# Moving the normalised row to PSUM, handing far adds to TensorE and cutting the last gate into quarters in a YOCO trunk with PEER experts

## The reference

```
h = rmsnorm(x, ffn_norm)                         # HP
a = einsum('tkd,td->tk', u[idx], h)              # 128 experts per token: the "dots"
x = x + einsum('tk,tkd->td', gate * gelu(a), v[idx])      # the "adds"
g = sigmoid(rmsnorm(x, ple_norm) @ ple_wg)       # the gate
x = x + g * (p @ ple_wp)
out = rmsnorm(x, final_norm)
```

## Time and profile before

| | us |
|---|---|
| median of 3 runs | 2817.46 |
| lowest and highest | 2817.01, 2819.46 |
| the profiled execution, its own time | 2819.06 |
| its span, first to last instruction | 2817.3 |
| busy in the span: PE, DVE, ACT, POOL | 2283.0, 2131.1, 1091.4, 1244.0 |
| mean granted TensorE clock | 0.94 |

### The profile page before, as it was taken

The page is one execution under the profiler, slowest core; times in us unless marked ns, Lnnn a source line. Parts: engine busy times, 40 slices in busy tenths (PEclk is TensorE's granted clock), DMA queues, the critical chain, the costliest instruction groups (busy, mean ns, idle before and its releaser), DMA issues.

```text
span 2817.3 us, 22875 instructions
## 1 busy us (share of the span) xinstructions
PE 2283.0 (81%) x6632; PEld 1170.4 (42%) x6632; DVE 2131.1 (76%) x4499; ACT 1091.4 (39%) x3193; POOL 1244.0 (44%) x1042
## 2 busy tenths in 40 slices
PE   7887669877799878887677898899867797768777
PEld 5545225342335534554253355456524342223222
DVE  5897888878777767768888887686797887675445
ACT  3442334324344334632324343363332435333333
POOL 2444444434444344543544544354343444444334
PEclk8999989999899999999889999899998999989999
DMA  9999999999999999999999999999999999999996
GB/s 363 415 402 420 420 420 419 419 416 420 417 394 420 420 420 414 419 420 420 420 418 418 416 380 420 419 410 420 420 420 419 419 410 420 420 400 421 419 420 267
DMA packets 163646, 1157.53 MB, mean 411 GB/s; under 512 B 18360, under 2 KB 20536, under 8 KB 26048
## 3 DMA queue, kind: packets, MB, share of 16 engines
q0 software_dynamic: 148416, 1073.81, 92.4%
q1 hardware_dynamic: 14528, 80.43, 7.0%
q10 hardware_dynamic: 576, 1.84, 0.2%
HBM read 1153.90 MB, written 2.10 MB: 410 GB/s over the span
## 4 chain that ended last, share of the span: by engine, by line
DMA 43%; PE 29%; DVE 19%; ACT 5%; issue 3%; POOL 1%; DVEq 0%; ACTq 0%; POOLq 0%
DMA slot<-in_uv,idx 42%; PE acc L1041 15%; DVE slot L1805 8%; DVE X L1793 2%; PE B L791 2%; PE M L663 2%; PE B L663 2%; POOL slot L631 1%; PE M L791 1%; ACT diag L1283 1%; PE M L982 1%; ACT w L1275 1%; PE B L982 1%; ACT act_a L1273 1%; DVE top_u L1417 1%
## 5 line engine op out<-in xcount | busy, mean ns | idle before, releaser
L1041 PE MATMUL acc<-slot,diag 128*128 128x512 f32 x2968 | 1509.5, 645 | 478.3 <-ACT diag L1283 477.3
L631 POOL DMA_INDIRECT slot<-in_uv,idx x1012 | 1212.2, 1198 | 1535.2 <-PE acc L1041 1082.5
L1805 DVE CUSTOM_DVE_ANT_0 slot<-slot,HP 128x1024 f32<-128x1024 f32 x1024 | 1242.0, 1220 | 535.1 <-DMA slot<-in_uv,idx 516.8
L1041 PEld LDWEIGHTS acc<-slot,diag 128*128 128x128 f32 x2968 | 557.4, 201 | 1316.9 <-ACT diag L1283 778.3
L1273 ACT ACTIVATE act_a<-a 128x1 f32<-128x1 f32 x1024 | 208.4, 204 | 1563.9 <-DVE a L1805 1557.8
L1793 DVE SCALAR_TENSOR_TENSOR X<-slot,w,X 128x1024 f32<-128x1024 f32 x276 | 353.6, 1281 | 13.3 <-ACT w L1275 13.2
L1275 ACT ACTIVATE w<-act_a,gate 128x1 f32<-128x1 f32 x1012 | 300.8, 297 | 33.0
L1283 ACT ACTIVATE diag<-cst,w 128x128 f32<-128x128 f32 x736 | 296.9, 403 | 23.8
L1805 DVE DVE_READ_ACCUMULATOR2_ANT a<- 128x1 f32 x1024 | 83.8, 82 | 0.0
L1273 ACT ACT_TABLE_LOAD x57 | 73.1, 1283 | 9.1 <-DVE a L1805 8.1
L791 PE MATMUL M<-TT,w 128*128 128x256 f32 x320 | 72.8, 384 | 0.0
(11 more groups left out here) (233 smaller groups left out, 1734.8 us busy)
## 6 DMA issues: line engine op xcount, KB each, us to landing
w<-in_wq SPq DMA_DIRECT2D x18, 1024.0 KB
slot<-in_uv,idx POOLq DMA_INDIRECT x1012
w<-in_w_o SPq DMA_DIRECT2D x8, 1024.0 KB
w<-in_w_dq SPq DMA_DIRECT2D x6, 1024.0 KB
w<-in_w_uq_nope SPq DMA_DIRECT2D x8, 768.0 KB
KV<-in_ple_wg SPq DMA_DIRECT2D x5, 1024.0 KB, 19.5
slot<-in_wq SPq DMA_DIRECT2D x4, 1024.0 KB, 12.5
KV<-in_wq SPq DMA_DIRECT2D x4, 1024.0 KB, 16.6
```

Of the source, the lines that this page charges most:

```text
L631: nc.gpsimd.indirect_dma_start(out=slot[s][:, 0:width], out_offset=None, in_=uv[g // NC] if n < GATHERS - LATE else near, in_offset=bass.I ...
L1041: last = nc.tensor.matmul(acc[:, half * 512:half * 512 + 512], diag[adds_on_pe(n) % DIAGS][:], slot[s][:, D + half * 512:D + half * 512 + ...
L1805: nc.vector.tensor_tensor_reduce(out=slot[s][:, 0:D], in0=slot[s][:, 0:D], in1=HP[:, :], scale=1.0, scalar=0.0, op0=ALU.mult, op1=ALU.add, ...
```

## The change

From row `HP_MOVES` = 936 on, ScalarE copies HP to the PSUM tile T, and the dots from row 945 on read T in place of HP. The near half of row 1023 is added by VectorE and not by TensorE. The far halves of rows 1017 and 1018 (`FAR_ON_PE`, 5 and 6) are gathered first and added by TensorE to the far half of `acc`, whose sum into X moves from before the last dot to the middle of the tail; VectorE makes the other ten far adds behind both copies of the first half's transposes. Transposes and their copies go in quarters of 256 columns, into the two halves of T in turn. The gate's columns go in three groups, 0:512, 512:768 and 768:1024, the last into `acc`; the sum of squares of the third group is made by VectorE, and the bias of the root in two steps. The diff leaves out the counts of semaphores per stage and the wider tile of single values.

```diff
@@ -54,6 +54,11 @@
 DESCRIPTORS = 2048
 ROWS = 64
 WARM, WARM_AGAIN, WARM_LAST = 11, 3, 5
+FAR_ON_PE = (5, 6)
+FAR_ORDER = FAR_ON_PE + tuple(i for i in range(LATE) if i not in FAR_ON_PE)
+HP_MOVES = GATHERS - KSEL + 40
+TAIL_COLUMNS = ((0, 512), (512, 768), (768, 1024))
+QUARTER_AT = (0, 512, 256, 768)
 STEP = "step"
 
 C_IDENT, C_MASK, C_IOTA, C_INV, C_EPS = 0, P, 2 * P, 2 * P + TOPK, 2 * P + TOPK + HALF
@@ -305,7 +310,7 @@
 def on_dve(n):
 
     g, k = divmod(n, KSEL)
-    return n < GATHERS - LATE and PLACED[g][1][k] == "D"
+    return n == GATHERS - 1 or (n < GATHERS - LATE and PLACED[g][1][k] == "D")
 
 
 DVE_DONE = [0]
@@ -543,6 +548,8 @@
         dve_steps = sem("dve_steps")
         half_summed, hat_scaled, half_gated, half_added = (sem("half_summed"), sem("hat_scaled"), sem("half_gated"),
                                                            sem("half_added"))
+        gate_sums = dict(zip(TAIL_COLUMNS, (M[:, 0:512], M[:, 512:768], acc[:, 0:256])))
+        hp_moved, columns_multiplied = sem("hp_moved"), sem("columns_multiplied")
         out_squared, out_biased, out_rooted = sem("out_squared"), sem("out_biased"), sem("out_rooted")
         trig_shifted, trig_done = sem("trig_shifted"), sem("trig_done")
         copied = (m_copied, b_copied)
@@ -634,7 +641,7 @@
                     ).then_inc(rows_loaded[s], 16)
             pool.wait_ge(weights_used, used("ple_wp", PAIRS - 2, 0))
             pool.wait_ge(last_embedded, 1)
-            for i in range(LATE):
+            for i in FAR_ORDER:
                 k = KSEL - LATE + i
                 nc.gpsimd.indirect_dma_start(
                     out=late_rows[i], out_offset=None, in_=far,
@@ -998,14 +1005,37 @@
             def tail_stage(g0, n):
                 t0 = before("t_copied", "tail", g0)
                 pe.wait_ge(t_copied, t0)
+                for i in FAR_ON_PE:
+                    pe.wait_ge(late_loaded[i], 16)
+                    nc.tensor.matmul(acc[:, 512:D], diag[adds_on_pe(GATHERS - LATE + i) % DIAGS][:], late_rows[i],
+                                     start=False, stop=(i == FAR_ON_PE[-1])).then_inc(pe_added, 1)
+                wg = [piece("ple_wg", g0, i) for i in range(4)]
+
+                def gated(k, lo, hi):
+
+                    at = (k % 4) * 512 + lo % 512
+                    return nc.tensor.matmul(gate_sums[lo, hi], TT[:, k, 0:P], wg[2 * (lo // 512) + k // 4][:, at:at + hi - lo],
+                                            start=(k == 0), stop=(k == DB - 1))
+
                 for half in range(2):
                     pe.wait_ge(half_summed, half + 1)
-                    transposes(X[:, g0 % NC, half * 512:half * 512 + 512], 4, at=half * 512).then_inc(t_filled, 1)
+                    for quarter in (2 * half, 2 * half + 1):
+                        at = quarter * GW
+                        transposes(X[:, g0 % NC, at:at + GW], 2, at=QUARTER_AT[quarter]).then_inc(t_filled, 1)
                     if half == 0:
-                        warm(5, M, ident)
-                    pe.wait_ge(t_copied, t0 + half + 1)
-                    for i in (half, half + 2):
-                        half_product(0, i, piece("ple_wg", g0, i)).then_inc(weights_used, 1)
+                        warm(2, M, ident)
+                        for quarter in range(2):
+                            pe.wait_ge(t_copied, t0 + quarter + 1)
+                            for lo, hi in TAIL_COLUMNS:
+                                for k in (2 * quarter, 2 * quarter + 1):
+                                    gated(k, lo, hi)
+                    else:
+                        for lo, hi in TAIL_COLUMNS:
+                            for k in range(4, DB):
+                                if lo == 0 and k % 2 == 0:
+                                    pe.wait_ge(t_copied, t0 + k // 2 + 1)
+                                last = gated(k, lo, hi)
+                            last.then_inc(columns_multiplied, 1)
                 yield
 
             def add_stage(g0, n):
@@ -1041,7 +1071,8 @@
                     last = nc.tensor.matmul(acc[:, half * 512:half * 512 + 512],
                                             diag[adds_on_pe(n) % DIAGS][:],
                                             slot[s][:, D + half * 512:D + half * 512 + 512],
-                                            start=(n == mine[0]), stop=(n == (whole if half else mine)[-1]))
+                                            start=(n == mine[0]),
+                                            stop=(n == (whole if half else mine)[-1] and not (half and g == PAIRS - 1)))
                 last.then_inc(pe_added, 1)
                 if n == GATHERS - WARM_LAST:
                     wait_mb("tail", PAIRS - 1, 1)
@@ -1234,20 +1265,20 @@
                 yield from norms("tail", g0, rows(g0, 1), D)
                 nc.scalar.activation(out_rms[:, 0:1], ident[:, 0:1], ACT.Sigmoid)
                 act.wait_ge(hat_scaled, 1)
-                for half in range(2):
-                    at = slice(half * 512, half * 512 + 512)
-                    act.wait_ge(weights_used, used("ple_wg", g0, 2 + half))
-                    nc.scalar.activation(A[:, 0, at], M[:, at], ACT.Sigmoid,
+                for j, (lo, hi) in enumerate(TAIL_COLUMNS):
+                    act.wait_ge(columns_multiplied, j + 1)
+                    nc.scalar.activation(A[:, 0, lo:hi], gate_sums[lo, hi], ACT.Sigmoid,
                                          scale=rstd[:, norm_number("tail", g0):norm_number("tail", g0) + 1]
                                          ).then_inc(half_gated, 1)
-                    if half:
-                        nc.scalar.activation(out_rms[:, 0:1], out_ss[:, 0:1], ACT.Sqrt)
-                    act.wait_ge(half_added, half + 1)
-                    nc.scalar.activation(sq_out[:, at], X[:, c, at], ACT.Square, accum_out=out_ss[:, half:half + 1]
-                                         ).then_inc(out_squared, 1)
-                    act.wait_ge(out_squared, half + 1)
-                act.wait_ge(out_biased, 1)
-                nc.scalar.activation(out_rms[:, 1:2], out_ss[:, 1:2], ACT.Sqrt, bias=out_bias[:, 0:1], scale=1.0 / D
+                    if j < 2:
+                        act.wait_ge(half_added, j + 1)
+                        nc.scalar.activation(sq_out[:, lo:hi], X[:, c, lo:hi], ACT.Square, accum_out=out_ss[:, j:j + 1]
+                                             ).then_inc(out_squared, 1)
+                act.wait_ge(out_squared, 2)
+                nc.scalar.activation(out_rms[:, 0:1], out_ss[:, 0:1], ACT.Sqrt)
+                act.wait_ge(out_squared, 3)
+                act.wait_ge(out_biased, 2)
+                nc.scalar.activation(out_rms[:, 1:2], out_ss[:, 2:3], ACT.Sqrt, bias=out_bias[:, 1:2], scale=1.0 / D
                                      ).then_inc(out_rooted, 1)
                 act.wait_ge(out_ready, NC)
                 act.dma_start(out[c * P:(c + 1) * P, 0:D // 2], outs[c][:, 0:D // 2]).then_inc(out_stored, 16)
@@ -1269,6 +1300,10 @@
                 s = n % SLOTS
                 if k in ranks_of(g):
                     act.wait_ge(gate_ready, before("idx_ready", ranks_of(g)[k], g) + 1)
+                if n == HP_MOVES:
+                    act.wait_ge(t_copied, before("t_copied", "tail", g))
+                    act.wait_ge(hp_ready, before("hp_ready", "renorm", g) + 1)
+                    nc.scalar.activation(T[:, :], HP[:, :], ACT.Copy).then_inc(hp_moved, 1)
                 act.wait_ge(dotted_or_added, DOTS[n])
                 nc.scalar.activation(act_a[:, s:s + 1], a[:, s:s + 1], ACT.Gelu_apprx_tanh).then_inc(gelued, 1)
                 act.wait_ge(gelued, n + 1)
@@ -1729,37 +1764,51 @@
                     return nc.vector.scalar_tensor_tensor(X[:, c, halves[1]], late_rows[i], weight_of(n),
                                                           X[:, c, halves[1]], ALU.mult, ALU.add)
 
-                for i in range(2):
-                    step(add_far(i))
+                near_half, far_half = halves
                 dve.wait_ge(pe_added, adds_on_pe(GATHERS - 1))
-                nc.vector.tensor_tensor(X[:, c, halves[0]], X[:, c, halves[0]], acc[:, halves[0]], ALU.add
-                                        ).then_inc(half_summed, 1)
-                for i in range(2, 4):
-                    step(add_far(i))
-                for half in range(2):
-                    dve.wait_ge(t_filled, before("t_filled", "tail", g0) + half + 1)
-                    nc.vector.tensor_tensor(TT[:, 4 * half:4 * half + 4, 0:P],
-                                            T[:, half * 512:half * 512 + 512].rearrange(blocks, t=P),
-                                            columns(G_PLE + DB + 4 * half, 4), ALU.mult).then_inc(t_copied, 1)
-                    if half == 0:
-                        for i in range(4, LATE - 1):
+                dve.wait_ge(dotted_or_added, added_by(GATHERS - 1))
```

(44 more changed lines are left out.)

8 lines of the change are left out of this document (4 added, 4 removed).

## The result

The changed kernel takes **2824.73 us**, the median of 12 runs (2821.43 to 2826.47); the kernel before, measured beside it, 2818.72 (12 runs, 2817.01 to 2820.49). The ratio is 1.0021 with a 95% interval of 1.0012 to 1.0029: slower by 6.0 us, just over the 5.6 us that the prediction set as the bound for no change. Forecast were 2818.6, a range of 2816.2 to 2821.6, and a chance of 0.05 for slower.

A forecast was written before the change was run, and what follows sets the result against it. Gathered rows (DMA) bound the kernel until the last rows are in, then VectorE's tail chain. Terms of +0.97 us (last dot to last far add's end) and +0.19 (to the root) took the median 2817.46 to 2818.6; range 2816.2 to 2821.6.

The forecast's parts named there:

- the terms of the sum: Tail behind the last dot: +0.97 us up to the last far add's end, +0.19 from there to the root; +1.2 together.
- part 1: HP's copy to PSUM at row 936 costs 0; dots reading PSUM cost 0, at most 0.1 us.
- freed, it would be some four us earlier. That is worth 0: GpSimd's last far issue in the tail comes some four us earlier, worth 0 as VectorE reaches that row after 2800.0.
- The first item of part 2: Behind the last dot, VectorE waits for TensorE's add of row 1022: start 2788.36, 1.12 long, so 2789.5.
- Rival (a): TensorE idles 2.5 us before the second products, clock falls to 0.50 for 3.4 us; 1.1 to 1.7 us lost; chance 0.33.
- Rival (e): Dots slower with an operand in PSUM, over the twelve near rows; slower by over 0.2%, 2828 at twice the length; chance 0.03.
- The ends of part 2: From the last dot to the last far add's end: near sum, copies, ten far adds at 0.88; end at 2802.4, +0.97 us.
- H: Instant the last far add ends, before which nothing of the last gate's second half can start; forecast 2802.4, +0.97 us.
- Part 3: From the last far add's end to ScalarE's last root, with quarters and three column groups: 12.14 against 11.95, +0.19 us.
- rival (b): Quarters in the tail leave only 256 columns' work behind the last product; 1.4 us less than before, 2817.0; chance 0.12.
- (c): Landings of far rows, not VectorE, set the last far add's end, and freed GpSimd pays; 2817.5 to 2818; chance 0.06.
- (d): HP's copy does not free GpSimd; last landing 2800.0, time 2818.6 as forecast; no chance of its own given.

The follow-up runs named there:

- e6: Changed kernel with twelve idle products keeping TensorE busy before the second half's transposes; 2820.09 us, ratio 1.0006.
- e5: Changed kernel, unaltered, measured again in the second group; 2821.44 us, ratio 1.0008.
- f1: Changed kernel, unaltered, measured again in the fourth group; 2824.62 us, ratio 1.0020.
- f5: f6 with far gathers 2 to 9 on GpSimd each held until a dot of rows 1016 to 1023 is done; 2819.62 us, ratio 1.0003.
- f6: The kernel of e6 again (changed kernel, TensorE kept busy by idle products), in the fifth group; 2823.97 us, ratio 1.0020.
- e3: Kernel before with only the move of HP to PSUM, late dots reading T; 2818.64 us, ratio 1.0003.
- e1: Changed kernel with all twelve far adds on VectorE, none on TensorE; 2822.35 us, ratio 1.0015.
- e2: Changed kernel with HP left in SBUF, all dots reading HP; 2820.38 us, ratio 1.0008.
- e11: Changed kernel with two far adds ahead of the first copies, HP in SBUF, ScalarE's squares behind the next sigmoid; 2817.74 us, ratio 0.9998.
- first and second group: Variants of the changed kernel taking parts back, then variants testing TensorE's granted clock, on one chip; kernel before 2818.29 and 2818.89 us.
- e8: Changed kernel with HP left in SBUF and idle products keeping TensorE busy before the second half; 2818.56 us, ratio 1.0000.
- f2: The kernel of e3 again (kernel before with only HP moved to PSUM), in the fourth group; 2821.97 us, ratio 1.0009.
- f3: Changed kernel with GpSimd holding each far gather until the one two before it has landed; 2830.39 us, ratio 1.0037.

## Why the prediction was wrong

An estimate of where the 6.0 us come from, from medians of the later groups: the terms of the sum, +1.2 (e6 against before, no pause and no clock fall); the clock fall, 1.35 (e5 against e6); the pause, 3.3 to 4.35 (f1 against e5, each over its own before; f5 against f6). Together 5.9 to 6.9. Of these differences only f5 against f6 is clear of the noise, and how the parts mix within the first twelve executions isn't shown: the one with a profile has the pause, and no lower clock over its second products.

- **The step that failed** is in part 1: "freed, it would be some four us earlier. That is worth 0", and with it "GpSimd's twelve far issues only change order" in the sum. The faster issues came exactly as forecast (0.95 long, 1.25 apart) and were worth nothing as a gain, also as forecast. No rival had GpSimd's pace as a harm. The runs put it at 3.3 to 4.35 us on such a chip and at nothing measurable on another (e3, 0.35). The first item of part 2, "so 2789.5" for TensorE's add, took the matmul's row as the time at which VectorE may go on, and 2791.34 came.
- **Rival (a)**, the granted clock, held: TensorE idle for 2.99 us (2.5 forecast), 0.50 for 3.41 us, 1.64 on the first sigmoid's path (1.1 to 1.7 forecast). In the first profile of the changed kernel the fall stands elsewhere: behind the pause's idle stretch of 3.18 us the clock was at 0.50 for 3.41 us, so the first eight passes of the first products took 4.54 us and the next eight 2.74. That shortened TensorE's idle stretch before the second transposes to 1.29, far adds covered the delay, and VectorE's wait for the sigmoid stayed at 2.64. f1, the same kernel, had an idle stretch of 3.26 there without a fall, and the fall in the second products (wait 4.33). An idle stretch should have been looked for ahead of both groups of products.
- **Rival (e)**, dots slower from PSUM, fell: 1221 ns (12 near rows: 1222), against 1220 before.
- **The ends of part 2** held where no pause was: in e5 the near sum comes 0.28 behind the dot's end (0.35 forecast), and H 13.23 behind it (13.25 forecast). Part of that is luck. The copies waited 0.84 us for transposes where the sum has 1.2. Against that, ten far adds took 9.1 us (9.08 in the first profile) and not 8.67, since the pause of 0.50 before one of them, which I left out, is there as before; it recurs in many of these kernels, at its own place (before the eighth of ten adds here, before the eighth of twelve in e1, nowhere in e2). By its profile e6 is 0.95 - 0.27 = +0.7 from the last dot's end to the root, so that its median stands at exactly +1.2 is luck too.
- **Part 3**: +0.19 forecast, -0.26 measured. The first sigmoid (H + 4.81) and the second (H + 7.70) stand within 0.06 of the forecast; what was mis-sized is the second group on VectorE and its square, H + 9.53 for the third sigmoid against 9.78, and the root's read-in behind its table, 11.40 against 11.84. So rival (b), quarters, was right in sign and worth a quarter us, not 1.4. What held it is the square before the next sigmoid, as argued: e11, where the squares stand behind it and the clock didn't fall, has the root at H + 11.16, 0.5 earlier than e6 (H + 11.68).
- **Rivals (c) and (d)** fell: the landings didn't set H in the changed kernel, and the copy did free GpSimd.

## What stays open

How a burst of gathers delays TensorE's increments isn't shown, nor why only some chips do it: it appeared in the first measurement and on three chips of the later groups, and in none of the six kernels with HP in PSUM on a fourth (first and second group). Each chip but that one ran one group, so the chip can't be told from the time of the measurement. One rival is untested: that the recording of the trace takes part. On the chip without the pause every trace holds 18105 landing records; all others hold 17443 to 17719, that of the kernel before too, and in the paused ones they are nearly gone while TensorE's increments are late (24 from 2780 to 2790 us in the first profile of the changed kernel, 167 in e5). Every execution on record has a span and a granted clock, so none shows these kernels without recording. What f5 and f6 show holds either way for the times measured here. Whether HP in PSUM costs something beyond the pace, neither: e8 (SBUF) is 1.5 us under e6 (PSUM), inside their intervals. f2 is 3.2 us over before, of which its profile shows 1.45 from the last dot's end to H (13.73 against 12.28). The version nearest to a gain is e11, 2817.74 against 2818.43, which can't be told from no change; no version was shown to beat the kernel before.

## What to carry to other kernels

Making an engine issue DMAs faster was not free of side effects here, though it gained nothing: where gathers that nobody waits for go out back to back, look at who waits for a counter at that time, and pace them by the work that consumes them, not by their landing. Where a change adds an idle stretch to TensorE, price the next products at both levels of its clock, and try idle products in it, sized so that they end before the work that follows. And measure on several chips: one kernel was 2.6 us over the kernel before on one and 5.9 on another, while the kernel before stood at the same time on each.

## What the runs showed of the hardware that was not expected

- Increments of TensorE's counter arrived some 3.6 us after the modelled end of their matmuls (after, f1, f6), and in a bunch 0.04 to 0.08 us apart, while GpSimd had issued twelve gathers 1.25 us apart. With the middle gathers 1.6 to 2.2 us apart (f5) they arrived one by one. ScalarE's gelu started on time behind each dot meanwhile: VectorE's increments were not held up.
- A far gather issued behind near ones took up to 12.9 us to land (f3: issued at 2778.06, the wait for it over at 2790.94), against 3.7 to 4.0 with the queue drained.
- With HP in PSUM an issue of GpSimd beside a dot took 0.95 us, and 1.62 with HP in SBUF. The Trainium skill (SBUF — State Buffer, section on who interferes with whom) says that a VectorE instruction with two SBUF inputs contends with a GpSimd instruction that reads SBUF: the trace agrees.
